# Reordering the row-sorting stage of a hybrid SSM, attention and MoE encoder layer on one Trainium2 core

## The reference

```python
h = rmsnorm(x, norm_mix_g[i]); proj = h @ w_in[i]
...
x = x + mixed @ w_out[i]
h = rmsnorm(x, norm_ffn_g[i]).reshape(bsz * s, d)
x = x + moe_ffn(h, w_router[i], ...).reshape(bsz, s, d)
gate = jax.nn.sigmoid(rmsnorm(x, norm_ple_g[i]) @ w_ple_gate[i])
x = x + gate * (p[i] @ w_ple_proj[i])
...
def moe_ffn(h, w_router, b_router, w_gu, b_gu, w_dn, b_dn):
    logits = (h @ w_router + b_router).astype(jnp.float32)
    top_val, top_idx = lax.top_k(logits, TOP_K)
    gates = jax.nn.softmax(top_val, axis=-1)
    # 4096 assignments grouped by expert; for each block of rows of expert e:
    act = clamped_swiglu(xb @ w_gu[e] + b_gu[e])
    y = act @ w_dn[e] + b_dn[e]
    # y times its gate, added to the token's row
```

## Time and profile before

| | us |
|---|---|
| Median of 3 runs (2425.56 to 2425.99) | 2425.62 |
| The profiled execution | 2425.37 |
| Its span | 2423.7 |
| PE busy | 2326.0 (96%) |
| DVE busy | 881.4 (36%) |
| ACT busy | 454.3 (19%) |
| POOL busy | 439.9 (18%) |
| DMA: 528.58 MB | mean 218 GB/s |

### The profile page before, as it was taken

One profiled execution on the slowest core, in us unless ns is written; L12 is line 12 of the kernel. 1 busy time (PEld: TensorE's weight loads), 2 busy tenths in 40 slices (PEclk: granted clock), 3 DMA queues, 4 the chain that ended last, 5 costly groups with the idle time before them and its releaser, 6 DMA issues.

```text
span 2423.7 us, 41324 instructions
## 1 busy us (share of the span) xinstructions
PE 2326.0 (96%) x15554; PEld 1639.1 (68%) x15555; DVE 881.4 (36%) x2033; ACT 454.3 (19%) x914; POOL 439.9 (18%) x710
## 2 busy tenths in 40 slices
PE   8999999999389999999999999999999999999898
PEld 5545566455245577887878878878888887767443
DVE  3644476233743433332333323322322222111364
ACT  3110165311011111111111111111111111100244
POOL 0445588000001111101011010101111000000320
PEclk9999999899689999999999999999999999999999
DMA  5100100300399999988889889867777666542540
GB/s 188 40 23 6 40 36 1 150 35 33 101 381 391 397 397 336 319 317 315 317 312 325 311 315 329 300 252 292 307 311 287 242 226 234 198 164 111 177 172 35
DMA packets 94254, 528.58 MB, mean 218 GB/s; under 512 B 16919, under 2 KB 17959, under 8 KB 42095
## 3 DMA queue, kind: packets, MB, share of 16 engines
q1 hardware_dynamic: 72143, 460.19, 50.9%
q0 software_dynamic: 22048, 67.53, 8.0%
HBM read 495.26 MB, written 31.23 MB: 217 GB/s over the span
## 4 chain that ended last, share of the span: by engine, by line
PE 91%; DVE 5%; ACT 2%; issue 1%; DMA 0%; POOL 0%; ACTq 0%; SPq 0%; DVEq 0%; POOLq 0%
PE ps L1763 37%; PE ps L1780 15%; PE ps L1820 5%; PE ps L1557 5%; PE ps L1842 3%; PE ps L1662 2%; PE ps L1547 2%; PE ps L1664 2%; PE ps L1797 2%; PE ps L1903 2%; PE ps L1719 1%; PE ps L1507 1%; PE ps L1576 1%; PE ps L1608 1%; PE ps L1594 1%; PE ps L1643 1%
## 5 line engine op out<-in xcount | busy, mean ns | idle before, releaser
L1763 PEld LDWEIGHTS ps<-xT,wg 128*128 128x128 f32 x6912 | 873.0, 191 | 26.6 <-issue 13.5
L1763 PE MATMUL ps<-xT,wg 128*128 128x128 f32 (+3 forms) x6912 | 889.1, 291 | 0.0
L1402 DVE TENSOR_SCALAR gb<-ps,bcur 128x256 f32<-128x256 f32 x216 | 104.4, 483 | 922.8 <-PE ps L1763 922.8
L1780 PE MATMUL ps<-wd,actT 128*128 128x512 f32 x864 | 375.6, 592 | 0.0
L1780 PEld LDWEIGHTS ps<-wd,actT 128*128 128x128 f32 x864 | 162.1, 190 | 193.7 <-issue 187.3
L855 ACT ACTIVATE sg<-gb 128x256 f32<-128x256 f32 x216 | 90.0, 417 | 785.9 <-DVE gb L1402 785.9
L1820 PE MATMUL ps<-wg,xT 128*32 128x256 f32 x2304 | 130.8, 383 | 7.1 <-ACT xT L784 7.1
L1903 PE MATMUL ps<-wpg,xnT 128*128 128x512 f32 x256 | 115.0, 605 | 5.9 <-ACT xnT L868 5.9
L1820 PEld LDWEIGHTS ps<-wg,xT 128*32 128x32 f32 x2304 | 73.2, 111 | 57.4 <-issue 10.4
L801 ACT ACTIVATE yb<-ps 128x512 f32<-128x512 f32 x54 | 31.2, 596 | 402.9 <-PE ps L1780 181.4
L1392 DVE TENSOR_TENSOR tb<-gb,sg 128x256 f32<-128x256 f32 x216 | 91.9, 425 | 34.8 <-ACT sg L855 34.8
(11 more groups left out here) (396 smaller groups left out, 2396.0 us busy)
## 6 DMA issues: line engine op xcount, KB each, us to landing
wg<-in_w_gu SPq DMA_DIRECT2D x264, 1024.0 KB, 6.8
wd<-in_w_dn SPq DMA_DIRECT2D x132, 1024.0 KB, 7.2
expert_rows<-yb POOLq DMA_DIRECT2D x48, 256.0 KB, 8.4
expert_rows<-yb POOLq DMA_DIRECT2D x60, 128.0 KB, 4.7
hT<-in_x_cm SPq DMA_DIRECT2D x8, 512.0 KB, 11.4
cumb<-gate_sums SPq DMA_DIRECT2D x4, 1024.0 KB, 4.7
x<-in_x_tm SPq DMA_DIRECT2D x1, 4096.0 KB, 13.4
wout<-in_w_out SPq DMA_DIRECT2D x1, 4096.0 KB, 20.9
```

The source lines that it names most:

```text
L1402: v.tensor_scalar(gb[:, f % 2, :], ps[:, f % 2, 0:W], bcur[:, f:f + 1], 7.0, ALU.add, ALU.min).then_inc(S("g_ready"), 1)
L1763: ins = m.matmul(ps[:, f % 2, g_ * W:g_ * W + w], wg[:, f, k, g_, :], xT[:, k, 0:w], start=(k == 0), stop=(k == KT - 1))
L1780: ins = m.matmul(ps[:, 2 + c, :], actT[:, f, 0:P], wd[:, c, f, :], start=(f == 0), stop=(f == FT - 1))
```

## The change

- Start: a small DMA brings the eight gain columns first; `w_u` comes in eight chunks, each behind its chunk of `hT`, and ACT waits for both; the rest of `par` comes after the fourth.
- The 16 one-column products of the start become 16 transposes of 128 columns; the 16 of the row squares become products with all 128 columns of `ones`, and they stand behind `project(0, 0)` and `project(0, 1)`. The router product takes 128 columns of its weights in place of 32, at a shifting place of the bank, so that the 32 right columns add up in columns 96 to 127.
- Sorting: `logits` keeps running sums `csel` per block, so that the chain of seven additions goes (PE adds them in by a `ones` product). The softmax stands ahead of the counting. `gsp` is made by POOL, and PE sums it over the four choices. The first expert's number is worked out as soon as the cut into passes is known, and SP loads its first four `wg` chunks then. ACT, not DVE, multiplies `ohc` by the token number and copies `smap`.
- Biases: 16 units, each a product of 32 rows (`gdT` by `b_dn`) and a product with the identity that adds `x1`; ACT copies each unit to `x1`. Six stand ahead of the list of tokens, three between its quarters, seven behind it. POOL clears the two tiles.
- End: ACT does `ple_norm(0)` ahead of the last four copies of the embedding projection.

```diff
+            sp.dma_start(par[:, 0:O_GSSM], small[:, 0:O_GSSM]).then_inc(S("gain_ld"), 16)
             for k in range(KT):
                 sp.dma_start(hT[:, k, :], x_cm[:, k, :]).then_inc(S(f"in_ld{k}"), 16)
-                if k == 0:
-                    sp.dma_start(par[:, :], small).then_inc(S("par_ld"), 16)
-                    sp.dma_start(w_u[:, 0:4, :], w_in[:, 0:4, 1544:2056]).then_inc(S("wu_ld"), 16)
+                sp.dma_start(w_u[:, k, :], w_in[:, k, 1544:2056]).then_inc(S(f"in_ld{k}"), 16)
...
+            sp.wait_ge(S("first_ready"), 1)
+            e0 = sp.value_load(first[0:1, 0:1], min_val=0, max_val=E - 1)
+            for f in range(4):
+                gu_chunk(e0, f)
             sp.wait_ge(S("tab_ready"), 1)
...
-            sp.wait_ge(S("id_mm"), 1)
-            for f in range(FT):
-                gu_chunk(e0, f)
+            sp.wait_ge(S("rows0_ld"), 16)
+            sp.wait_ge(S("rows1_ld"), 16)
+            for f in range(4, FT):
+                gu_chunk(e0, f)
...
-                        ins = m.matmul(ps[:, 6, c:c + 1], toks, ident[:, 0:1], start=True, stop=True)
+                        ins = m.transpose(ps[:, (0, 1, 6, 7)[c // 4], (c % 4) * P:(c % 4) * P + P], toks, ident)
...
+            def row_squares():
+                pe.wait_ge(S("sqs_ready"), 6)
+                pe.wait_ge(S("sqa_ready"), 3)
+                for c in range(16):
+                    sq = sqs[:, 0, c * P:c * P + P] if c < 8 else sqat[:, (c - 8) * P:(c - 7) * P]
+                    ins = m.matmul(ps[:, 4 + c // 4, (c % 4) * P:(c % 4) * P + P], sq, ones[:, :], start=True, stop=True)
+                ins.then_inc(S("ss_mm"), 1)
...
+            pe.wait_ge(S("ssm_ready"), 8)
             pe.wait_ge(S("out_ld"), 48)
-            pe.wait_ge(S("sm_ready"), 1)
             project(0, 0)
             project(0, 1)
+            row_squares()
+            pe.wait_ge(S("sm_ready"), 1)
...
+            def bias(un):
+                i, n, j = un // 8, un // 4 % 2, un % 4
+                if un >= 4:
+                    pe.wait_ge(S("wo_evac"), 13 + un)
+                bank = ps[:, 2 + j, :]
+                m.matmul(bank, gdT[32 * j:32 * j + 32, i, :], bdn[32 * j:32 * j + 32, 512 * n:512 * n + 512], start=True, stop=False, skip_group_check=True)
+                m.matmul(bank, ident, x1[:, 4 * i + j, 512 * n:512 * n + 512], start=False, stop=True, skip_group_check=True).then_inc(S("wo_mm"), 1)
...
+            dve.wait_ge(S("id_mm"), 1)
+            v.tensor_copy(rowid[:, :], ps[:, 1, P - nh:P]).then_inc(S("rowid_ready"), 1)
...
             for i in range(16):
+                if i == 12:
+                    ple_norm(0)
                 act.wait_ge(S("pp_mm"), i + 1)
                 a.activation(ple_in[:, i // 2, 512 * (i % 2):512 * (i % 2) + 512], ps[:, 4 + i % 4, :], ACT.Copy).then_inc(S("pp_evac"), 1)
-            ple_norm(0)
```

More of the change, by code:

```diff
@@ L157, in build @@
         rowc = sb("rowc", [P, 2], U32)
+        first = sb("first", [1, 1], I32)
         passtab = sb("passtab", [P, 4], I32)
@@ L259, in build @@
         slf = at("slf", [P, 32], F32, o); o += 128
+        csel = at("csel", [P, 9, 32], F32, R_V + 32768)
+        before = at("before", [1, 32], F32, R_V + 33920)
         assert o <= R_S
@@ L280, in build @@
         bcur = at("bcur", [P, 24], F32, o); o += 96
-        gsp = at("gsp", [P, 8, TOPK, 32], F32, R_S + 28672)
+        gsp = at("gsp", [P, TOPK, 8, 32], F32, R_S + 28672)
         bb = at("bb", [64, 2, 2, 256], F32, R_S + 28672)
@@ L1194, in _ @@
             dve.wait_ge(S("ss_mm"), 1)
[L1195 removed]
+            v.tensor_scalar(rss[:, :].rearrange("p (b c) -> p b c", b=4), ps[:, 4:8, 0:512:P], 1.0 / 512, EPS, ALU.mult, ALU.add).then_inc(S("sm_ready"), 1)
             dve.wait_ge(S("sd2_ready"), 1)
@@ new lines, in _ @@
+            pe.wait_ge(S("cs_ready"), 8)
+            m.matmul(ps[:, 1, 256:384], ones[:, :], cf_[:, 160:288], start=True, stop=True, skip_group_check=True).then_inc(S("cnt_mm"), 1)
+            m.matmul(ps[:, 0, 0:256], tri, sel[:, :, :].rearrange("p t e -> p (t e)"), start=False, stop=True, skip_group_check=True).then_inc(S("cnt_mm"), 1)
+            pe.wait_ge(S("gs_ready"), 1)
+            for i in range(2):
+                for k in range(TOPK):
+                    ins = m.matmul(ps[:, 7, i * P:i * P + P], gsp[:, k, 4 * i:4 * i + 4, :].rearrange("p t e -> p (t e)"), ident,
+                                   start=(k == 0), stop=(k == TOPK - 1), skip_group_check=True)
@@ L1703, in _ @@
+            for un in range(6):
+                bias(un)
             for q in range(4):
-                pe.wait_ge(S("hot_ready"), q + 1)
+                pe.wait_ge(S("tok_ready"), 2 * q + 2)
                 for c in range(8 * q, 8 * q + 8):
-                    ins = m.matmul(ps[:, 1, 0:2 * MAXPASS + 4], ohr[:, c, :], ohc[:, c, :], start=(c == 0), stop=(c == 31))
+                    nh = 2 * MAXPASS + 4
+                    at_, lo = (P - nh, 0) if c == 0 else (0, nh * c + nh - P)
+                    ins = m.matmul(ps[:, 1, at_:at_ + P], ohr[:, c, :], ohc[:, :, :].rearrange("p c n -> p (c n)")[:, lo:lo + P],
+                                   start=(c == 0), stop=(c == 31), skip_group_check=True)
+                if q < 3:
+                    bias(6 + q)
@@ L1707, in _ @@
             ins.then_inc(S("id_mm"), 1)
-            pe.wait_ge(S("tab_ld"), 16)
-            ends = [pe.value_load(passrow[0:1, 4 * c + 3:4 * c + 4], min_val=c + 1, max_val=MAXPASS) for c in range(NW)]
-            npass = ends[NW - 1]
+            for un in range(9, 16):
+                bias(un)
             def turn_half(a_):
@@ L1728, in turn_rows_in @@
                     turn_half(1)
[L1730 to L1745 removed]
+            pe.wait_ge(S("tab_ld"), 16)
             pe.wait_ge(S("rows0_ld"), 16)
@@ L1749, in _ @@
             pe.reg_load(n_next, passrow[0:1, 2:3])
+            pe.wait_ge(S("wo_evac"), 32)
             turn_rows_in(n_next)
-            bias(2)
-            bias(3)
+            ends = [pe.value_load(passrow[0:1, 4 * c + 3:4 * c + 4], min_val=c + 1, max_val=MAXPASS) for c in range(NW)]
+            npass = ends[NW - 1]
             def expert_pass(b, w):
```

163 lines of the change are left out of this document (78 added, 85 removed).

## The result

| | before | changed |
|---|---|---|
| median of the runs | 2425.59 us (6 runs, 2423.64 to 2426.23) | 2414.91 us (6 runs, 2398.55 to 2416.06) |
| ratio, 95% interval | | 0.9945 [0.9929, 0.9962] |
| mean granted clock | 0.978 to 0.980 | 0.994 in the run of 2398.55, 0.986 to 0.988 in the others |

The change wins 10.7 us where 27.6 were forecast, and 2414.9 lies above the range of 2387 to 2411. The six times don't form one group: one execution takes 2398.55, and the other five 2411.75 to 2416.06, with a lower mean clock. I read both kinds.

The account below looks back on a forecast made before the run. PE was taken as busy everywhere but about 606 to 727 us, plus chains of waits at start and end. Gains of 8.4 + 1.0 + 10.7 + 7.5 = 27.6 us gave a median of 2398, range 2387 to 2411.

Parts of the forecast that it names:

- the clock's rise on the way: Sorting on PE: 0.8 us allowed for the clock coming up during the first six bias units, which end at 632.8.
- rival 1: PE's clock stays low through the sorting stage: first pass at 701, 24.5 later than before, kernel 2439; 4 in 100.
- Start: Chain of waits at the start: transposes, no clock fall and earlier data win 8.4 us (4 to 9.5).
- Row squares: Row squares moved behind the first two projections: 1.0 us won, between 0 and 4.8.
- The wider router product costs nothing: Router product of 128 instead of 32 columns: no added time, 16 instructions already taking 1.71 us with 32.
- Gates and first unit: Sorting: `gates` ready at 613.2, then `gsp`, its turn and a copy; the first bias unit can start at 620.0.
- A unit: Sorting on PE: one bias unit takes 2.0 us (1.1 to 2.4), including 0.28 for changing between 32 and 128 rows.
- The list: Sorting: after six units, four quarters and three more units, the token list is ready at 647.4, near where it was.
- Five loads bare: PE's five loads of pass bounds, covered before, stand uncovered ahead of the first expert pass: 3.5 us.
- First pass: First expert pass starts at 665.9 instead of 676.57: sorting wins 10.7 us, with bounds of 4 and 17.5.
- Chunks: First four weight chunks lie ready; the other four land by 668, needed near 676: hidden, 8 us to spare.
- End: Final chain: earlier `ple_norm(0)` brings the turn and first gate product forward, 7.5 us won (5 to 8).

Follow-up runs that it names:

- usual execution: Changed kernel unaltered, lower mean clock: most of its executions, 2411.75 to 2416.06 us; its profile, from a second run of the same file, has span 2414.8.
- quick execution: Changed kernel unaltered, the one execution of 2398.55 us with a mean clock of 0.994; its first profile, span 2397.0.
- experiment 2: Changed kernel with each unit's bias product over all 128 rows instead of 32 (bias output wrong): 2392.87 us, ratio 0.9867.
- experiment 5: Changed kernel with bias units in groups of four: four 32-row products side by side, then four identity products: 2390.44 us, ratio 0.9857.
- experiment 6: On top of experiment 5, PE's five loads of pass bounds put ahead of its wait for the gathered rows: 2393.42 us, ratio 0.987.
- experiment 9: Changed kernel with the start's 16 one-column products put back in place of the 16 transposes: 2420.85 us, ratio 0.9983.
- experiment 4: Changed kernel with both products of a bias unit over the same 32 rows, no switch (output wrong): 2422.47 us, ratio 0.9991.
- experiment 10: Changed kernel with all eight first weight chunks asked for behind the gathered rows, instead of four early: 2417.71 us, ratio 0.9963.
- experiment 8: Kernel before with only `ple_norm(0)` moved ahead of ACT's last four copies at the end: 2417.58 us, ratio 0.9966.
- experiment 3: Changed kernel with each unit's bias product over 64 rows instead of 32, switch kept (bias output wrong): 2416.42 us, ratio 0.9957.
- experiment 1: Changed kernel run once more, unaltered, for a second profile: 2414.27 us, ratio 0.995.

## Why the prediction was wrong

**The failed step** is in the sorting on PE: "Six units, with 0.8 for the clock's rise on the way, end at 632.8", and with it the argument against rival 1, "long products without gaps brought the clock up within 6 us in each place". The places it was taken from had products of all 128 rows. The units are gapless work too, PE 10.00 of 10.00 from 620 to 630, but half their instructions put 32 rows to work, and the clock stays at 0.50 from 605 until it comes up at 645, in the second of the list's quarters, which are shorter products but all of 128 rows. What was put at 0.8, the clock's rise on the way, cost 16.0. Seven units at 4.00 instead of 2.11 make 13.3, two quarters (3.78 + 2.47 for 2.05 + 1.78) 2.4, the turn of `gsp` 0.3. In the usual execution the first pass comes 18.3 later than in the quick one (674.10 and 655.79): 2.3 of that is there before the gates' turn (605.88 and 603.60), and the other 16 are these three.

**Rival 1 was this mechanism,** at 4 chances in 100. Its price was too high: a first pass 24.5 later than before, where the usual one is 2.5 earlier. It priced a low clock for three quarters and more of the 37 us of work; in fact nine of the sixteen units ran at the full one. The point from which it was to decide was set wrong as well, and so was its reason: it saw PE's idle time ahead as the cause, and behind the same idle time the clock was up within 1 us of the first product with full rows or of the first group of four (experiments 2, 5 and 6).

The other steps, by the quick execution where the clock is as the forecast had it:

- *Start:* 8.4 forecast; 7.8 in the quick profile, 8.0 in the usual one. Undone alone in part (experiment 9) it costs 6. Right.
- *Row squares:* 1.0 forecast, 0 to 4.8 as bounds; 2.8 in the quick execution, 2.8 less 1.6 in the usual one. The fall ahead of the projections cost 1.9 (5.37 for 3.43) and not 2.8. Another 1.5 and 1.1 were won ahead of it, in the attention, for which the forecast had no term; in experiment 4's profile nothing was won there (the gate products end 7.6 earlier, after 8.0 from the start). Why isn't shown. That the clock could fall a second time, behind the row squares, the forecast had named; in the usual execution it did.
- *The wider router product costs nothing:* 1.78 for 1.71 per 16 instructions. Right.
- *Gates and first unit:* first unit at 620.0 forecast; 607.56 + 12.05 won ahead of it = 619.6. Right.
- *A unit:* 2.0 forecast, 2.11 at the full clock. Right, with the switch at 0.39 in place of 0.28. Of the two rules of the Trainium skill weighed there, the first (TensorEngine Tiling, Key Properties) says that a change of mode drains the engine; the runs show its price, 0.19, and not the draining itself. The second (TensorE: Matmul & The Clock Gate, Why this matters for your kernels) is borne out by experiments 2, 4 and 5: a 32-row product takes the 0.86 of a 128-row one, and four together take 1.07.
- *The list,* 647.4 forecast in the time of before, is 635.77 in the quick execution; with the 12.05 won ahead of it, that is 647.8. *Units end* at 661.4 forecast, 650.53 + 12.05 = 662.6. *Five loads bare:* 3.5 forecast, 2.80. All right.
- *First pass:* 665.9 forecast, 655.79 + 12.05 = 667.8. The turn of the rows with ACT's copies takes 1.8 (651.16 to 652.99), for which the forecast left 0.3. So the sorting stage wins 8.7 even with the clock up, for 10.7 forecast. That the first pass is still 20.8 earlier, for 20.1, is luck: the attention and the row squares gave 3.3 more than was forecast, against 0.6 less at the start and 2.0 less in the sorting.
- *Chunks:* asked for at 612.97 in the usual profile, with no wait for them ahead of the first pass; experiment 10 shows that they would be awaited otherwise.
- *End:* 7.5 forecast, 7.8 alone (experiment 8). In the usual execution the embedding product starts 1.5 earlier than before and the span is 8.9 shorter, so 7.4.

So the usual sum is 2.5 at the first pass, 1.0 of it lost in the passes (the first takes 13.08 for 12.15, at the low clock for longer), and 7.4 at the end: 8.9 between the spans of the two profiles. Of the 17.6 that are missing at the first pass, 16.0 are this one term.

The quick execution is no proof that the forecast was right. Of 26 executions of the changed kernel (10) and of its variants in experiments 9 and 10 (16), 2 are quick. In the profiles, where the clock was up when the first unit came, it stayed up through all sixteen; where it wasn't, the first seven units didn't raise it. What decides it in the 3.5 us of the turn of `gsp` ahead of them I haven't shown.

What stays open: whether, in the changed kernel, the switches add to what the few rows do. Experiment 4 shows that few rows suffice; 64 rows with the switch (experiment 3) could be held down by either. 64 rows without a switch were not tried.

## What to carry to other kernels

Price a small product at both clocks before it replaces work on another engine: 512 columns over 32 rows took as long here as over 128 (0.86 us both), and held the clock down, so a long stretch of it can run at half speed with PE never idle. Put narrow products side by side on different quarters of the rows, and all of one kind together, instead of one narrow product ahead of each full one: here that was worth 24.5 us, clock and price together. And where a forecast rests on "the clock comes up", look for rows in which it came up behind the same shape of product; if there are none, the chance of the other case isn't 4 in 100.

## What the runs showed of the hardware

- The clock follows more than PE's busy share. In six gapless units of one 32-row and one 128-row product, 24 us long, the granted clock stayed at 0.50 (experiment 1), and it fell from 1.00 to 0.50 in the second of seven gapless units of 32-row products alone (experiment 4); with 128 rows (experiment 2), or with four 32-row products at once (experiments 5 and 6), it was up 0.9 us into the first of them.
- At the full clock the same units don't bring it down: sixteen of them, with the list between, ran at 1.00 in the quick execution. So the same program has two times, 2398.6 and 2415, in the profiles by what the clock was at its first unit.
- The change between 32-row and 128-row products costs 0.19 us each time at the full clock (1.05 against 0.86) and 0.29 at the low one (2.00 against 1.71).
- The clock falls in one-column products though PE goes from one to the next (busy 1.00, granted clock 1.00 at 35 us and 0.50 from 37, experiment 9), and the work behind them pays: 9.96 for 6.99. 16 transposes of 128 columns in the same place leave it at 1.00, but they take only 1.75 us, so this doesn't tell whether they would keep it up for longer.
